# Seven block products for contraction steps 0 to 5 of the mix projection, a third weight sum on GpSimd

## The chip, the cores and the metric

One NeuronCore of a Trainium2 chip runs the whole program. The metric is the device time of one execution in microseconds (us). The kernel before was run three times; the profiled execution is a run of its own.

## The reference, cut to what matters

One decoder layer on 512 tokens and a model width of 1024, all in float32. The stage that changes is the last projection of the mixer, and the residual sum and norm behind it:

```python
merged = g[:, :, 0] * (o_a @ w_a) + g[:, :, 1] * (o_b @ w_b) + g[:, :, 2] * (o_c @ w_c)
return merged @ w_out
...
x = layer_norm(ALPHA * x + h, ln1_g[l], ln1_b[l])
h = memory_cross_attention(x, mem, w_xq[l], w_xkv[l], w_xo[l])
```

`merged` is 512 x 1024, `w_out` (`w_mix_out`) is 1024 x 1024. Every product is made in three matmuls: each float32 operand is split into a rounded part (`hi`) and the remainder (`lo`), and hi x hi, lo x hi and hi x lo are added up.

## The kernel before, in words

The layer is one program without a planner: each engine has its own written order, and semaphores tie the orders together. P = 128 rows are a tile; 512 tokens are four row blocks (t = 0 to 3), 1024 features are eight steps (k = 0 to 7).

Ahead of the mix run four gate iterations (`gate_iteration`, PE L2727, ACT L1279, DVE L1906). Each takes six gate pieces (q = 0 to 5) and two pieces of branch projections (q = 6, 7), every piece 24 matmuls of 512 columns. ScalarE rounds a weight piece of 1024 columns into `w_hi` (`gate_split`, L1305), VectorE makes the remainder into `w_lo` (`gate_rest`, L1901), TensorE multiplies, ScalarE takes the sigmoid into `sg`, and VectorE multiplies the three branches by their gates (L1922, L1923, L1929), adds them up (L1932, L1935) and splits the result into `m_hi` and `m_lo` (L1937, L1939), two steps k an iteration. A weight piece has a number p; `piece_done` counts the pieces that TensorE has used up, `lo_done` those whose remainder is made.

The mix product takes pieces PM to PM + 7, one for each step k. ScalarE rounds them (`split`, L1138), VectorE makes the remainders (`rest_of`, L1592), both on 1024 columns. TensorE (L2804 to L2827) begins with steps 0 and 1 over all row blocks, row blocks 2 and 3 first, since the last gated tiles are still being made, and then does steps 2 to 7 row block by row block (`rows_tail`, L2767). The product fills all eight PSUM banks, `2 * t + n` for row block t and column half n.

When a row block is complete, VectorE adds ALPHA times the residual input with a row sum (`norm_sums`, L1957), forms the mean (L1963), multiplies by gamma (`norm_gamma`, L1986), ScalarE sums the squares (L1321, L1324), GpSimd takes the root (L1112), and VectorE ends the norm (`norm_end`, L1995). TensorE then turns the normed block by eight small matmuls (`turn_tile`, L2437), ScalarE and VectorE split the turned tile into `xt_hi` and `xt_lo` (L1144, L1598). The turns of blocks 0 to 2 lie between the rows of later blocks, that of block 3 behind the memory keys (pieces PKX and PKX + 1, `tile_piece`, 24 matmuls of 256 columns each). Then come the cross attention's queries (`query`), which need the turned tiles.

SyncE issues all loads in one order (`load`, L886; the residual input L939; gamma and beta L941). Two raw buffers hold two pieces each. GpSimd has no work between the mixer's attention and the norms but the roots; in the first feed-forward product it makes one weight difference for each block (`weight_sums`, L1101).

The two feed-forward products are already made by seven block products. There `OUT_BANKS`, `out_slot` (half buffers of `w_hi` and `w_lo`), `LO` and `HI` (the lower and upper 256 tokens) and `OUT_PRODUCTS` are defined; the changed kernel uses them too. Some lines of the mix stage on TensorE:

```python
for k in range(2):
    pe.wait_ge(lo_done, PM + k + 1)
    for t in pair:
        for n in range(2):
            ins = rows_part(PM + k, k, t, n, m_hi, m_lo, k == 0, False)
...
rows_tail(PM, KT, N_TAIL, 0, m_hi, m_lo, lambda k: pe.wait_ge(merge_step, 6 * (k + 1)))
```

## Time and profile before

| what | value |
|---|---|
| three runs | 873.24, 873.60, 873.79 us; median 873.6 |
| profiled execution | 873.84 us, its span 872.1 us |
| TensorE (PE) matmul busy | 861.3 us, 99% of the span |
| VectorE (DVE) busy | 553.1 us, 63% |
| ScalarE (ACT) busy | 372.4 us, 43% |
| GpSimd (POOL) busy | 81.2 us, 9% |
| HBM traffic | 103 GB/s over the span |

The span runs from the first to the last instruction; 1.74 us of the device time lie around it. PE's matmuls overlap, so a matmul of 512 columns is shown with 389 ns, while the next one starts 227 ns after it: the pace is read from starts. In the timeline, `x2` marks two instructions merged into one row, and the bracket behind a row is the idle time before it with what ended it.

### The profile page before, as it was taken

The numbers are of one execution on the slowest core, as the hardware profiler recorded it, in microseconds if no ns is written. First come the engines' busy times: TensorE is split into PE (matmuls) and PEld (weight loads), VectorE is DVE, ScalarE is ACT, GpSimd is POOL, SyncE is SP. The second block draws the span as 40 slices with busy tenths as digits, with TensorE's granted clock in tenths as the row PEclk, the third lists the DMA queues.
The fourth block names the chain that finished last, engine by engine and source line by source line (L and its number), as shares of the span: only waits on it lengthen the run. The fifth ranks groups of instructions, "written<-read, shape, count | busy, mean of one in ns | idle before, by whom it ended". The sixth has DMA issues, their size and how long they took to land.

```text
span 872.1 us, 13309 instructions
## 1 busy us (share of the span) xinstructions
PE 861.3 (99%) x5143; PEld 747.3 (86%) x5143; DVE 553.1 (63%) x1016; ACT 372.4 (43%) x747; POOL 81.2 (9%) x103
## 2 busy tenths in 40 slices
PE   9999999999999999999999999999999999999996
PEld 8988888877678888888889979899999999888785
DVE  4344347769632626262767579679888888877934
ACT  4112157229642222222324554355656556434511
POOL 3100000081310000000000000011111111000000
PEclk9999999999999999999999999999999999999999
DMA  8534530430003333236531311313332333751101
GB/s 289 165 97 132 134 98 25 145 93 6 1 2 97 97 97 96 96 96 235 190 105 66 129 49 49 97 49 110 127 104 97 98 97 105 266 210 48 49 25 72
DMA packets 71832, 90.36 MB, mean 104 GB/s; under 512 B 3149, under 2 KB 62359, under 8 KB 71775
## 3 DMA queue, kind: packets, MB, share of 16 engines
q1 hardware_dynamic: 71391, 89.15, 31.3%
q8 instruction: 38, 0.62, 0.3%
q0 software_dynamic: 384, 0.43, 0.3%
q14 instruction: 19, 0.16, 0.1%
HBM read 87.05 MB, written 2.52 MB: 103 GB/s over the span
## 4 chain that ended last, share of the span: by engine, by line
PE 94%; DVE 3%; issue 1%; DMA 1%; ACT 1%; SPq 0%; DVEq 0%; POOLq 0%; POOL 0%; ACTq 0%
PE ps L2400 19%; PE ps L2402 19%; PE ps L2401 19%; PE ps L2970 7%; PE ps L2972 7%; PE ps L2971 7%; PE ps L2565 3%; PE ps L2642 3%; PE ps L2602 3%; PE ps L3028 1%; PE ps L3029 1%; PE ps L3030 1%; PE ps L2437 1%; DMA x_nat<-in_x 1%; PE ps L3073 1%
## 5 line engine op out<-in xcount | busy, mean ns | idle before, releaser
L2400 PE MATMUL ps<-xt_hi,w_hi 128*128 128x512 f32 (+1 forms) x400 | 155.6, 389 | 0.3 <-DVE w_lo L2110 0.3
L2402 PE MATMUL ps<-xt_lo,w_hi 128*128 128x512 f32 (+1 forms) x400 | 154.8, 387 | 0.0
L2401 PE MATMUL ps<-xt_hi,w_lo 128*128 128x512 f32 (+1 forms) x400 | 154.8, 387 | 0.0
L1138 ACT CAST w_hi<-raw 128x1024 fp32r<-128x1024 f32 (+1 forms) x49 | 50.5, 1035 | 133.3 <-PE ps L2402 121.6
L1901 DVE TENSOR_TENSOR w_lo<-raw,w_hi 128x1024 fp32r<-128x1024 f32 x30 | 36.7, 1224 | 90.1 <-ACT w_hi L1305 90.1
L2400 PEld LDWEIGHTS ps<-xt_hi,w_hi 128*128 128x128 f32 x400 | 75.1, 188 | 16.1 <-issue 1.1
L2402 PEld LDWEIGHTS ps<-xt_lo,w_hi 128*128 128x128 f32 x400 | 75.1, 188 | 15.4
L2401 PEld LDWEIGHTS ps<-xt_hi,w_lo 128*128 128x128 f32 x400 | 75.1, 188 | 15.1
L1592 DVE TENSOR_TENSOR w_lo<-raw,w_hi 128x1024 fp32r<-128x1024 f32 (+1 forms) x49 | 59.1, 1207 | 39.1 <-ACT w_hi L1138 38.9
L2971 PE MATMUL ps<-xt_hi,w_lo 128*128 128x256 f32 x288 | 81.5, 283 | 0.0
L2972 PE MATMUL ps<-xt_lo,w_hi 128*128 128x256 f32 x288 | 81.5, 283 | 0.0
L2970 PE MATMUL ps<-xt_hi,w_hi 128*128 128x256 f32 x288 | 81.5, 283 | 0.0
L2970 PE MATMUL ps<-s_hi,w_hi 128*128 128x256 f32 x216 | 61.3, 284 | 0.4 <-DVE w_lo L2144 0.3
L2971 PE MATMUL ps<-s_hi,w_lo 128*128 128x256 f32 x216 | 61.1, 283 | 0.0
L2972 PE MATMUL ps<-s_lo,w_hi 128*128 128x256 f32 x216 | 61.1, 283 | 0.0
L2144 DVE TENSOR_TENSOR w_lo<-raw,w_hi 128x512 fp32r<-128x512 f32 x72 | 49.9, 705 | 16.9 <-ACT w_hi L1416 16.6
L2971 PEld LDWEIGHTS ps<-xt_hi,w_lo 128*128 128x128 f32 x288 | 55.3, 192 | 0.1
L2970 PEld LDWEIGHTS ps<-xt_hi,w_hi 128*128 128x128 f32 x288 | 55.3, 192 | 0.1
L2972 PEld LDWEIGHTS ps<-xt_lo,w_hi 128*128 128x128 f32 x288 | 55.3, 192 | 0.0
L1291 ACT ACTIVATE sg<-ps,bias_t 128x512 f32<-128x512 f32 x24 | 16.6, 690 | 88.2 <-PE ps L2402 88.2
L1416 ACT CAST w_hi<-raw 128x512 fp32r<-128x512 f32 x72 | 44.3, 622 | 7.8 <-PE ps L2972 4.5
L1101 POOL TENSOR_TENSOR w_t<-raw 128x512 f32<-128x512 f32 x18 | 28.7, 1594 | 176.2 <-DMA raw<-in_w_ffn_in 151.9
(391 smaller groups left out, 1979.1 us busy)
## 6 DMA issues: line engine op xcount, KB each, us to landing
raw<-in_w_in SPq DMA_DIRECT2D x24, 1024.0 KB, 5.0
raw<-in_w_ffn_in SPq DMA_DIRECT2D x36, 512.0 KB, 4.4
raw<-in_w_ffn_out SPq DMA_DIRECT2D x7, 1024.0 KB, 4.8
raw<-in_w_mix_out SPq DMA_DIRECT2D x4, 1024.0 KB, 4.9
raw<-in_w_ffn_in SPq DMA_DIRECT2D x4, 1024.0 KB, 5.3
out_w<-in_w_ffn_out SPq DMA_DIRECT2D x4, 1024.0 KB, 8.8
raw<-in_w_branch_b SPq DMA_DIRECT2D x4, 512.0 KB, 3.9
resid<-in_x SPq DMA_DIRECT2D x1, 2048.0 KB, 9.5
```

Of the source, the lines that this page charges most:

```text
L1101: pool.tensor_tensor(w_t1[:, :, :], w_quarter(n, 0, 1), w_quarter(n, 0, 0), ALU.subtract).then_inc(t1_done, 1)
L1138: act.copy(hi, src).then_inc(hi_done, 1)
L1416: act.copy(op_slot(m, 0), right_operand(kind, n)).then_inc(op_hi, 1)
L1592: dve.tensor_tensor(lo, src, f32(hi), ALU.subtract).then_inc(lo_done, 1)
L1901: dve.tensor_tensor(w_lo[s][:, :].rearrange("p (k c) -> p k c", k=KT), v, f32(w_hi[s][:, :]).rearrange("p (k c) -> p k c", k=KT), ALU.subt ...
L2144: dve.tensor_tensor(op_slot(m, 1), right_operand(kind, n), f32(op_slot(m, 0)), ALU.subtract).then_inc(op_lo, 1)
L2400: pe.matmul(dst, a_hi, b_hi, start=start, stop=False, skip_group_check=reopened)
L2401: pe.matmul(dst, a_lo, b_hi, start=False, stop=False, skip_group_check=reopened)
L2402: return pe.matmul(dst, a_hi, b_lo, start=False, stop=stop, skip_group_check=reopened)
L2970: pe.matmul(dst, w_h[:, k, :], x_h[:, k, :], start=clear and k == 0, stop=False, skip_group_check=True)
L2971: pe.matmul(dst, w_l[:, k, :], x_h[:, k, :], start=False, stop=False, skip_group_check=True)
L2972: ins = pe.matmul(dst, w_h[:, k, :], x_l[:, k, :], start=False, stop=k == 3, skip_group_check=True)
```

## The change

Steps 0 to 5 of the contraction are no longer eight block products of (256 tokens x 3 steps) by (3 steps x 512 columns), but seven. Even steps (0, 2, 4) are the first block row of the weight, odd steps the second. Sums of the left blocks (S1 to S4, rounded into `n1`, `n3`, `n2` and in place of the block of P3) are made on VectorE and ScalarE in the last gate iteration, when steps 0 to 5 of `m` are complete. Four quarters of the weight rows 0 to 767 come by loads of their own into `mix_b` and `mix_w`. VectorE makes the weight sums T1, T2 and the fourth (into T2's place), 1536 columns each; GpSimd makes the third, T3, in three parts of 512 columns, once P5's remainders are made. Each right part of 512 columns is rounded by ScalarE (`mix_round`) and gets its remainder from VectorE (`mix_rest`), 21 of each in place of six pieces of 1024 columns. Between products ScalarE copies two banks into two others twice (`mix_seeds`, `mix_second_seeds`); VectorE adds the banks of P5 and P6/P7 to ALPHA times the residual (`keep_scaled`), so the last column half's norm sum takes the residual unscaled. Steps 6 and 7 stay plain (`rows_tail` over two steps) and P4 comes between the row blocks 1 and 2. On VectorE the last gate iteration is written out: its gate products go into `sg`, and its adds and splits stand between the remainders. On SyncE the residual load waits for P1's remainders and the third weight sum, gamma and beta for P7. The turn of block 2 moves behind the first memory-key piece, and `rest_of(PKX)`, `rest_of(PKX + 1)` and `rest_of(PXQ)` move into the norms. Piece numbers and waits behind the mix are renumbered.

```diff
+        MIX_T1 = raw[0][:, 0:N_MIX * 512].rearrange("p (k c) -> p k c", k=N_MIX)
+        MIX_B11, MIX_B12 = mix_b[:, 0, :, :], mix_b[:, 1, :, :]
+        MIX_B22, MIX_B21, MIX_T2, MIX_T3 = (mix_w[:, i, :, :] for i in range(4))
+        MIX_RIGHT = {"P1": MIX_B11, "P2": MIX_B21, "P3": MIX_B22, "P5": MIX_T1, "P6": MIX_T2, "P7": MIX_T3, "P4": MIX_T2}
...
+            sp.wait_ge(m_sum_lo, 4)
+            mix_quarter(MIX_B12, 0, 1).then_inc(mix_in, 16)
+            mix_quarter(MIX_B11, 0, 0).then_inc(mix_in, 16)
+            sp.wait_ge(piece_done, (N_PAIR - 1) * 8 + PG + 6)
+            mix_quarter(MIX_B22, 1, 1).then_inc(mix_in2, 16)
+            mix_quarter(MIX_B21, 1, 0).then_inc(mix_in2, 16)
             for c in range(CM, CF):
+                if c == CM + 1:
+                    sp.wait_ge(mix_lo, mix_op("P1", N_MIX))
+                    sp.wait_ge(mix_t3, N_MIX)
+                    sp.dma_start(resid[:, :, :], A["x"][0].rearrange("(t p) n -> p t n", p=P)).then_inc(resid_in, 16)
+                    sp.wait_ge(mix_lo, mix_op("P5", N_MIX))
                 load(c)
-                if c == CM:
-
-                    sp.wait_ge(o_ab_lo, N_OUT_AB)
-                    sp.wait_ge(o_lo_done, KT - N_OUT_AB)
-                    sp.dma_start(resid[:, :, :], A["x"][0].rearrange("(t p) n -> p t n", p=P)).then_inc(resid_in, 16)
+                if c == CM + 1:
+                    sp.wait_ge(mix_prod, mix_op("P7", N_MIX))
...
+            pool.wait_ge(mix_lo, mix_op("P5", N_MIX))
+            for k in range(N_MIX):
+                pool.tensor_tensor(MIX_T3[:, k, :], MIX_B22[:, k, :], MIX_B12[:, k, :], ALU.subtract).then_inc(mix_t3, 1)
...
+                if m < 4:
+                    act.wait_ge(piece_done, PM - 1 + m // 2)
+                else:
+                    act.wait_ge(mix_prod, m - 3)
+                act.copy(out_slot(m, 0), MIX_RIGHT[kind][:, k, :]).then_inc(mix_hi, 1)
...
+            for kind in OUT_PRODUCTS:
+                for k in range(N_MIX):
+                    if (kind, k) != ("P1", 0):
+                        mix_round(kind, k)
+                    if kind == "P7" and k in (0, 2):
+                        split(PM + k // 2)
+                if kind == "P5":
+                    mix_seeds()
+                if kind == "P2":
+                    mix_second_seeds()
...
+            m_add(M_D, "P4")
+            m_add(M_C, "P3")
+            dve.wait_ge(m_whole, 2)
+            dve.tensor_tensor(M_D, M_C, M_D, ALU.add).then_inc(m_sum, 1)
+            m_add(M_A, "P1")
+            gate_rest(LAST_I, 3, 0)
+            dve.wait_ge(m_whole, 3)
+            dve.tensor_tensor(M_C, M_A, M_C, ALU.subtract).then_inc(m_sum, 1)
+            dve.wait_ge(m_sum, 2)
+            dve.tensor_tensor(M_A, M_D, M_A, ALU.subtract).then_inc(m_sum, 1)
+            m_add(M_B, "P2")
+            dve.wait_ge(m_whole, 4)
+            dve.wait_ge(m_sum, 3)
+            dve.tensor_tensor(M_B, M_B, M_A, ALU.subtract).then_inc(m_sum, 1)
+            gate_rest(LAST_I, 4, 0)
+            for kind in ("P5", "P7", "P6", "P3"):
+                m_rest(kind)
+            gate_rest(LAST_I, 5, 0)
...
+            dve.wait_ge(mix_in, 32)
+            dve.wait_ge(lo_done, 8 * LAST_I + PG + 6)
+            dve.tensor_tensor(MIX_T1, MIX_B12, MIX_B11, ALU.subtract).then_inc(mix_t, 1)
+            gate_rest(LAST_I, 7, 0)
+            dve.wait_ge(piece_done, PM - 1)
+            dve.wait_ge(sig_done, N_PAIR * 6)
+            gate_product(6, 0).then_inc(merge_step, 1)
+            gate_product(7, 2).then_inc(merge_step, 1)
+            gate_product(0, 4).then_inc(merged_even, 1)
+            mix_rest("P1", 0)
+            mix_rest("P1", 1)
+            dve.wait_ge(mix_in2, 32)
+            dve.wait_ge(mix_t, 1)
+            dve.tensor_tensor(MIX_T2, MIX_B22, MIX_T1, ALU.subtract).then_inc(mix_t, 1)
+            dve.wait_ge(piece_done, PM)
+            gate_product(2, 3).then_inc(merge_step, 1)
+            mix_rest("P1", 2)
+            gate_product(1, 1).then_inc(merge_step, 1)
+            gate_product(3, 5).then_inc(merged_odd, 1)
+            for k in range(N_MIX):
+                mix_rest("P5", k)
+            for k in range(N_MIX):
+                mix_rest("P6", k)
+            dve.wait_ge(merge_step, merged_so_far + 4)
+            dve.wait_ge(merged_even, N_PAIR)
+            add_gated(0, True)
+            dve.wait_ge(merge_step, merged_so_far + 5)
+            add_gated(0, False)
+            mix_rest("P2", 0)
+            split_gated(0)
+            mix_rest("P2", 1)
+            dve.wait_ge(merged_odd, N_PAIR)
+            add_gated(1, True)
+            mix_rest("P2", 2)
+            dve.wait_ge(merge_step, merged_so_far + 9)
+            add_gated(1, False)
+            dve.wait_ge(mix_lo, mix_op("P6", N_MIX))
+            dve.tensor_tensor(MIX_T2, MIX_B21, MIX_T2, ALU.subtract).then_inc(mix_t, 1)
+            mix_rest("P7", 0)
+            rest_of(PM)
+            mix_rest("P7", 1)
+            split_gated(1)
+            mix_rest("P7", 2)
+            dve.wait_ge(resid_in, 16)
+            dve.wait_ge(mix_prod, mix_op("P5", N_MIX))
+
+            def keep_scaled(t, bank):
+
+                v = resid[:, t, 512:1024]
+                dve.scalar_tensor_tensor(out=v, in0=v, scalar=ALPHA, in1=ps[:, bank, :], op0=ALU.mult,
+                                         op1=ALU.add).then_inc(mix_kept, 1)
+
+            for r in range(2):
+                keep_scaled(r, 5 + 2 * r)
+            mix_rest("P3", 0)
+            rest_of(PM + 1)
+            mix_rest("P3", 1)
+            mix_rest("P3", 2)
+            dve.wait_ge(mix_prod, mix_op("P7", N_MIX))
+            for r in range(2):
+                keep_scaled(2 + r, 4 + 2 * r)
+            for k in range(N_MIX):
+                mix_rest("P4", k)
...
             norm_sums(0)
-            norm_out(0)
+            norm_gamma(0)
+            rest_of(PKX)
+            norm_end(0)
             norm_sums(1)
-            norm_out(1)
+            norm_gamma(1)
+            rest_of(PKX + 1)
+            norm_end(1)
             turn_tile(1, 0)
             norm_sums(2)
             norm_out(2)
             turn_tile(1, 1)
-            norm_sums(3, (0,))
+            norm_sums(3)
+            norm_gamma(3)
+            rest_of(PXQ)
+            norm_end(3)
             turn_tile(1, 2)
-            norm_sums(3, (1,))
-            norm_out(3)
-            rest_of(PXQ)
             rest_of(PXQ + 1)
...
+                def part(k, r):
+
+                    m = mix_op(kind, k)
+                    pe.wait_ge(mix_lo, m + 1)
+                    w_h, w_l = out_slot(m, 0), out_slot(m, 1)
+                    rows = slice(P * r, P * r + P)
+                    dst = ps[:, OUT_BANKS[kind][r], :]
+                    clear = kind in ("P1", "P5") and k == 0
+                    pe.matmul(dst, x_h[:, k, rows], w_h, start=clear, stop=False, skip_group_check=True)
+                    pe.matmul(dst, x_l[:, k, rows], w_h, start=False, stop=False, skip_group_check=True)
+                    return pe.matmul(dst, x_h[:, k, rows], w_l, start=False, stop=k == N_MIX - 1, skip_group_check=True)
+
+                if kind == "P1":
+                    for k in range(N_MIX):
+                        part(k, 0)
+                    pe.wait_ge(merge_step, 2 * N_PAIR * 6 - 9)
+                    for k in range(N_MIX):
+                        part(k, 1).then_inc(mix_prod, 1)
                 else:
-                    pe.wait_ge(merged_odd, N_PAIR)
-                for k in range(2):
-                    pe.wait_ge(lo_done, PM + k + 1)
-                    for t in pair:
-                        for n in range(2):
-                            ins = rows_part(PM + k, k, t, n, m_hi, m_lo, k == 0, False)
-                    if pair[0] == 0:
-                        ins.then_inc(piece_done, 1)
-            rows_tail(PM, KT, N_TAIL, 0, m_hi, m_lo, lambda k: pe.wait_ge(merge_step, 6 * (k + 1)))
-            rows_tail(PM, KT, N_TAIL, 1, m_hi, m_lo)
+                    for k in range(N_MIX):
+                        part(k, 0)
+                        part(k, 1).then_inc(mix_prod, 1)
+
+            for kind in OUT_PRODUCTS[:-1]:
+                mix_product(kind)
+            mixed = PM - 2 * N_MIX
+            rows_tail(mixed, KT, KT - 2 * N_MIX, 0, m_hi, m_lo,
+                      lambda k: pe.wait_ge(merge_step, 2 * N_PAIR * 6 - 4 * (KT - 1 - k)))
+            rows_tail(mixed, KT, KT - 2 * N_MIX, 1, m_hi, m_lo)
+            mix_product(OUT_PRODUCTS[-1])
             turn_tile(1, 0)
-            rows_tail(PM, KT, N_TAIL, 2, m_hi, m_lo)
+            rows_tail(mixed, KT, KT - 2 * N_MIX, 2, m_hi, m_lo)
             turn_tile(1, 1)
-            rows_tail(PM, KT, N_TAIL, 3, m_hi, m_lo, halves=(0,))
-            rows_tail(PM, KT, N_TAIL, 3, m_hi, m_lo, halves=(1,), part=slice(0, 2))
-            turn_tile(1, 2)
-            rows_tail(PM, KT, N_TAIL, 3, m_hi, m_lo, halves=(1,), part=slice(2, None))
+            rows_tail(mixed, KT, KT - 2 * N_MIX, 3, m_hi, m_lo)
 
             pe.wait_ge(mem_lo, 4)
             pe.wait_ge(turn_lo, 2 * TT + 2)
             for n in range(2):
                 pe.wait_ge(lo_done, PKX + n + 1)
                 tile_piece(PKX + n, n, memt_hi, memt_lo, slice(0, MEM))
+                if n == 0:
+                    turn_tile(1, 2)
             turn_tile(1, 3)
```

## Rows read from the trace of the kernel before

**Rows 1.** The page: granted clock by slice, and the chain that ended last.
```profile
PEclk9999999999999999999999999999999999999999
...
PE 94%; DVE 3%; issue 1%; DMA 1%; ACT 1%; SPq 0%; DVEq 0%; POOLq 0%; POOL 0%; ACTq 0%
```
**Rows 2.** PE's groups by form, 420.96 to 474.1: count | busy us, mean ns | idle.
```profile
L2400 PE MATMUL ps<-x_hi,m_hi 128*128 128x512 f32 x32 | 12.7, 398 | 0.0
```
**Rows 3.** PE in order of time, mix to queries: start, duration in us, line.
```profile
420.97 0.39 PE L2400 MATMUL ps<-w_hi,m_hi 128*128 128x512 f32 x1
421.19 0.39 PE L2401 MATMUL ps<-w_hi,m_lo 128*128 128x512 f32 x1
...
423.46 0.39 PE L2402 MATMUL ps<-w_lo,m_hi 128*128 128x512 f32 x1
423.87 0.50 PE L2400 MATMUL ps<-w_hi,m_hi 128*128 128x512 f32 x1
...
467.56 0.28 PE L2400 MATMUL ps<-memt_hi,k_hi 128*128 128x256 f32 x1
...
474.11 0.36 PE L2400 MATMUL ps<-xt_hi,c_hi 128*128 128x256 f32 x1
```
**Rows 4.** DVE in order of time, the last two merges.
```profile
416.93 1.22 DVE L1592 TENSOR_TENSOR w_lo<-raw,w_hi 128x1024 fp32r<-128x1024 f32 x1
418.07 0.68 DVE L1929 TENSOR_TENSOR mt<-ps,sg 128x512 f32<-128x512 f32 x1
418.67 0.68 DVE L1932 TENSOR_TENSOR mt<-mt 128x512 f32<-128x512 f32 x1
419.38 0.69 DVE L1935 TENSOR_TENSOR mt<-mt 128x512 f32<-128x512 f32 x1
420.11 0.43 DVE L1937 CAST m_hi<-mt 128x512 fp32r<-128x512 f32 x1
420.57 0.69 DVE L1939 TENSOR_TENSOR m_lo<-mt,m_hi 128x512 fp32r<-128x512 f32 x1
...
422.60 1.22 DVE L1592 TENSOR_TENSOR w_lo<-raw,w_hi 128x1024 fp32r<-128x1024 f32 x1
```
**Rows 5.** DMA issues, KB, us to landing; first three issued at 402.3 to 404, last 475.5.
```profile
raw<-in_w_mix_out SPq DMA_DIRECT2D x1, 1024.0 KB, 4.9
...
resid<-in_x SPq DMA_DIRECT2D x1, 2048.0 KB, 9.5
...
gb<-in_ln_b SPq DMA_DIRECT2D x1, 512.0 KB, 11.6
...
gb<-in_ln_b SPq DMA_DIRECT2D x1, 512.0 KB, 7.7
```
**Rows 6.** POOL in order of time, first feed-forward product.
```profile
591.53 1.30 POOL L1101 TENSOR_TENSOR w_t<-raw 128x512 f32<-128x512 f32 x1 [6.82 <-DMA raw<-in_w_ffn_in]
601.78 1.71 POOL L1101 TENSOR_TENSOR w_t<-raw 128x512 f32<-128x512 f32 x1 [8.95 <-DVE w_lo L2144]
```
**Rows 7.** DVE in order of time at the same places.
```profile
591.57 1.81 DVE L2158 TENSOR_TENSOR w_t<-raw,w_t 128x512 f32<-128x512 f32 x1
...
601.65 0.68 DVE L2194 TENSOR_TENSOR h_lo<-ht,h_hi 128x512 fp32r<-128x512 f32 x1
602.25 1.78 DVE L2158 TENSOR_TENSOR w_t<-raw,w_t 128x512 f32<-128x512 f32 x1
```
**Rows 8.** DVE in order of time: the norms of row blocks 2 and 3.
```profile
457.79 0.69 DVE L1957 SCALAR_TENSOR_TENSOR resid<-resid,ps 128x512 f32<-128x512 f32 x1 [2.74 <-PE ps L2402]
...
458.77 1.28 DVE L1986 SCALAR_TENSOR_TENSOR norm_part<-resid,neg_mean,gb 128x1024 f32<-128x1024 f32 x1
461.02 1.28 DVE L1995 SCALAR_TENSOR_TENSOR resid<-norm_part,rstd,gb 128x1024 f32<-128x1024 f32 x1 [0.96 <-POOL rstd L1112]
462.22 1.28 DVE L1598 TENSOR_TENSOR xt_lo<-ps,xt_hi 128x512 fp32r<-128x512 f32 x2
...
471.01 1.28 DVE L1995 SCALAR_TENSOR_TENSOR resid<-norm_part,rstd,gb 128x1024 f32<-128x1024 f32 x1 [0.99 <-POOL rstd L1112]
```

More of the change, by code:

```diff
@@ L1284, in gate_iteration @@
                     if last and q == 7:
-                        split(PM)
+                        mix_round("P1", 0)
                     elif not (first and q == 0):
                         gate_split(i, np_ - PG, wrap)
+                    if last and q == 3:
+                        for kind in ("P5", "P7", "P6", "P3"):
+                            m_round(kind)
                     if q < 6:
@@ L1310, in _ @@
             gate_iteration(N_PAIR - 1, True)
-            for p in range(PM + 1, PM + 8):
-                split(p)
+            for kind in OUT_PRODUCTS:
[6 more added lines that the diff above has]
+                    mix_seeds()
+                if kind == "P2":
+                    mix_second_seeds()
             act.wait_ge(merge_step, 2 * N_PAIR * 6)
@@ L1939, in gate_iteration, with m_add @@
                         dve.tensor_tensor(ml, mt[:, 0, :], f32(mh), ALU.subtract).then_inc(merge_step, 1)
-            gate_iteration(0, False)
+            gate_iteration(0)
             with dve.Fori(1, N_PAIR - 1) as i:
-                gate_iteration(i, False)
-            gate_iteration(N_PAIR - 1, True)
+                gate_iteration(i)
+            M_A, M_B, M_C, M_D = (m_sums[:, i, :, :] for i in range(4))
+            LAST_I = N_PAIR - 1
+            def m_add(dst, kind):
+                dve.tensor_tensor(dst, f32(m_left(kind, 0)), f32(m_left(kind, 1)), ALU.add).then_inc(m_whole, 1)
@@ L1956, in norm_sums @@
                     v = resid[:, t, c * 512:(c + 1) * 512]
-                    dve.scalar_tensor_tensor(out=v, in0=v, scalar=1.0 if n >= 2 * TT else ALPHA, in1=ps[:, 2 * t + c, :],
+                    scaled = n >= 2 * TT or n < TT and c == 1
+                    dve.scalar_tensor_tensor(out=v, in0=v, scalar=1.0 if scaled else ALPHA, in1=ps[:, 2 * t + c, :],
                                              op0=ALU.mult, op1=ALU.add,
@@ L2011, in turn_tile @@
                     turn_drain(2 * t + hf, 2 * TT * k + 2 * t + hf)
-            for p in range(PM + 2, PKX + 2):
-                rest_of(p)
             def memory_key_out(n):
```

156 lines of the change are left out of this document (125 added, 31 removed).

## The prediction

> **What bounds the kernel now.** I read the page first: TensorE holds 94% of the chain that ended last, at a granted clock of 9 tenths or more in every slice [rows 1]; the table above has it busy 99% of the span. So one question decides: how long TensorE takes from its first mix matmul to the first query matmul. What follows is untouched and moves with it. The groups of TensorE's lines in that stretch show six groups of mix matmuls like the one here, 6 x 32 = 192 [rows 2]. TensorE's order of time gives the ends: the mix begins at 420.97, the memory keys at 467.56, the queries at 474.11, 53.1 us in all [rows 3]. Matmuls with 512 columns start 0.227 us apart (420.97, 421.19). There is one stall: from 423.46 to 423.87, where 0.227 is due, behind the VectorE subtraction that ended at 422.60 + 1.22 = 423.82 [rows 3, 4]. It and the slow starts after it cost 0.3; about 0.12 of that is the restart itself, my price for each further one.
>
> **What goes.** The plain product has 192 matmuls. The changed one has 7 products x 3 steps x 2 row halves x 3 = 126, and keeps 2 x 4 x 2 x 3 = 48 for steps 6 and 7, together 174. 18 x 0.227 = 4.1 us go, and the old stall of 0.3: with nothing in its way TensorE would need 53.1 - 4.4 = 48.7 us.
>
> **What comes, walked engine by engine.** VectorE's durations, start to start: an operation on 512 columns 0.60 (418.07 to 418.67), on 1024 columns 1.14 (416.93 to 418.07), so 0.87 for 768 and 1.67 for 1536; one that needs the result before it 0.71 (418.67 to 419.38); a copy of 512 columns 0.46 (420.11 to 420.57) [rows 4].
>
> *Last gate iteration, 384 to 421.* Eight sums of 768 columns and four remainders come onto VectorE, 12 x 0.87 = 10.4 us, and four roundings onto ScalarE. VectorE has one rest of 1.14 in each 5.44 us of TensorE there (24 matmuls), so they fit between. The two pairs of weight quarters are 1.5 MB each; 1 MB landed after 4.9 us, 2 MB behind another 1 MB after 9.5 [rows 5]. Asked for at about 400.4 and 410.3 and priced between, at 7.2, they are in at 407.6 and 417.5; wanted at 407.7 and 418.7; at 9.5 only the second is late, and by 0.3 past the pause that follows. Taken at nothing.
>
> *Start of the mix.* P1's third right part can be rounded only when the last gate piece leaves its slot, 421.15, and VectorE first has a gate product (to 421.8). The part is there at 422.5, wanted at 422.3. Cost 0.2.
>
> *GpSimd's sums.* P5's last remainder ends at 426.2 and releases three GpSimd subtractions of 512 columns. Alone one takes 1.30 (591.53) [rows 6]. What it does beside VectorE stands in the trace: VectorE's subtraction of two SBUF tensors at 591.57 takes 1.81 where 0.69 is usual, the one at 602.25 takes 1.78, and GpSimd's of 601.78 (1.71) had itself stood behind VectorE's of 601.65 [rows 6, 7]. So a subtraction with two SBUF inputs loses 1.12 us when a GpSimd one has just begun, and the engines take turns. VectorE has only such work then: remainders for P6, adds, remainders for P2. The first GpSimd sum (426.3 to 427.5) falls into a pause of VectorE; the second and third (begun about 428.0 and 429.7) each hold up a remainder. Cost on VectorE 2 x 1.12 = 2.2.
>
> The Trainium skill (SBUF — State Buffer, section "SBUF: two separate sides") calls the port pair of VectorE and GpSimd an exclusive lock, held for a whole instruction, against VectorE operations with two SBUF inputs too. By that rule the sums cost the same 2.2, and the trace agrees (1.81 against 0.69); if the engines did not block each other it would be nothing, the first rival.
>
> *To P7.* From 427.4 VectorE has no pause: P6's remainders 1.8, two adds 1.3, P2's remainders 1.8, the even gate's split 1.1, two adds 1.2, the fourth sum 1.7, P7's first remainder 0.7, together 9.6. It ends at 427.4 + 2.2 + 9.6 = 439.2. One part of P2 is 0.2 late on the way. TensorE wants P7's at 420.97 + 4 x 4.08 + 0.2 + 0.2 + two restarts = 438.0. Cost 0.2 + 1.2.
>
> *P7 and P3.* Between six remainders VectorE has two rests of 1.14, a split of 1.1 and two scaled keeps of 0.6. By these durations four parts come 0.25, 0.2, 0.3 and 0.25 late. Cost 1.0. The restarts so far, seven at 0.12, are 0.8. The first keep also waits for the residual input, whose load now stands behind the third GpSimd sum: asked for at 431.0, it takes 4.9 to 9.5 [rows 5], so it is in by 440.5, wanted at 442.5. Covered by 2 us. The first cross-attention load queues behind it on SyncE's queue (431.5, wanted at 448.5), the second behind gamma and beta (445.5, wanted at 466.8); behind GpSimd's sums stands only the first norm's root (454). All covered.
>
> *The norms.* TensorE ends the first block of plain rows at 420.97 + 6 x 4.08 + 9 x 0.227 + the stalls 2.6 + restarts 0.8, and 0.2 for the last matmul to run out = 451.1. From there VectorE has for each row block: two sums and a mean 1.6 (0.61, then 457.79 to 458.77), gamma 1.3 (458.77 takes 1.28), the end 1.2 (461.02 to 462.22) [rows 8], 4.1 in all, four times 16.5; three weight rests that the change puts in between, 3.4; two turned tiles of two halves, 2.4; one wait for the root, 0.96 (461.02) [rows 8]. That is 23.3 us without a pause: the last block is normed at 474.4. TensorE's own way from the same matmul: 0.7 for the other half of block 0, 2.7 for block 1, P4 4.1, 5.4 for blocks 2 and 3, and for memory keys and turns what they took before: 6.55 from 467.56 to 474.11 with one turn of 0.8 [rows 3], so 5.75 and three turns 2.4, together 21.1, and 0.1 for slow starts, from 450.9 to 472.1. Before, VectorE ended its last norm at 471.01 + 1.28 = 472.3, a turn (0.8) and a full 1.0 ahead of the query at 474.11 [rows 3, 8]. Now it is the later one. Cost 2.2. The first query also needs the low part of the third tile, which VectorE makes only after that norm: 0.2, and a restart 0.1.
>
> Gamma and beta are asked for when P7 ends, the second at 444.8. It landed 7.7 us after its issue with 1 MB ahead, 11.6 with 3 MB ahead [rows 5]; nothing is queued ahead of it now, so I take at most 7.7: in by 452.5, wanted at 452.9. Counted at nothing; each microsecond over is paid in full.
>
> **Sum.** 48.7 + 0.2 + 0.2 + 1.2 + 1.0 + 0.8 + 2.2 + 0.2 + 0.1 = 54.6. Some ten hand-overs between engines are in the walk at 0.03; the one of 423.82 to 423.87 is 0.05, so 0.2 more: 54.8. Against 53.1 that is +1.7. The profiled execution took 873.84 us (span 872.1 and 1.74 around it), 0.24 above the median of the three runs, 873.6. 873.84 + 1.7 = 875.5; against the median it would be 875.3.
>
> **Rivals.** *GpSimd costs nothing.* Its sums fall into pauses or do not block: P7 begins on time and all that follows is 1.9 us earlier, 873.6, no change. Against it the rows of 1.8 us; for it, that no row has three GpSimd operations in a row.
> *VectorE keeps up.* If its lane through the norms is 2 us shorter than counted and P7 and P3 get their parts in time, 0.2 to 1.5 us of stalls are left: 873.84 - 4.4 + 1.5 = 871. For it: TensorE's chain share of 94% shows helpers hidden nearly everywhere, and the lane is long, so small errors add up. Against it: the lane is counted from rows, and it has no pause to lose.
> *A late load* (slower by a mechanism of its own). VectorE waits in order for the residual and for gamma and beta, with every remainder and norm queued behind. It decides if the residual takes over 11.5 us, or gamma and beta over 8.1 from the second issue, 0.4 above the row. At the 11.6 once seen it is 3.5 late: 879; at half of that 877.5.
> *Steps 0 to 5 stay eight products.* The code's loops say otherwise; under 1 in 100.
>
> **How the numbers follow.** Forecast 875.5: 0.50, its own range 874.4 to 876.9. GpSimd free, 873.6: 0.20. VectorE keeps up, 871: 0.15. Late load, 877.5 to 879: 0.15. Leaving out about a tenth at either end: 872.2 to 878.3. This kernel can be told from no change by about 0.2%, 1.75 us: faster is below 871.85, slower above 875.35. Of the forecast's 0.50 some 0.32 lies above 875.35; with the late load slower is 0.47. Faster is 0.14 of the 0.15. No difference is the rest, 0.39.
>
> **What would show it.** In the changed profile: VectorE subtractions of about 1.8 us near 428 to 431 beside GpSimd's; TensorE idle some 1.2 us before P7's first part, behind VectorE; tenths before P7's and P3's later parts; about 2.2 us before the last turn, behind the last norm's end; the queries at about 475.8. If no subtraction there exceeds 0.7, GpSimd is free. If gamma's row is late with a DMA as releaser, it is the late load. If TensorE idles under 2 us in all between 421 and 475, I counted VectorE too long and the forecast is wrong.

## The result, and the profile after

The changed kernel takes 879.53 us (median of four runs, 878.64 to 880.22) against 873.69 of the kernel before on the same chip: a ratio of 1.0062, 95% interval [1.0046, 1.0078]. It is slower by 5.8 us. The forecast was 875.5, with a range up to 878.3. The profiled execution took 878.64 us, its span is 876.9.

The page of the changed kernel, its chain that ended last by engine (before: [rows 1]):

```profile
PE 87%; DVE 7%; issue 2%; ACT 2%; DMA 1%; POOL 1%; SPq 0%; DVEq 0%; POOLq 0%; ACTq 0%
```

TensorE held 94% of the chain and now holds 87%; VectorE went from 3% to 7%. The kernel lost time not in matmuls but in waits for VectorE. TensorE in order of time, changed kernel: start, duration in us, line, and in brackets the idle time and its releaser (before: [rows 3]):

```profile
421.06 0.39 PE L3064 MATMUL ps<-w_hi,m_hi 128*128 128x512 f32 x1
...
438.19 0.39 PE L3066 MATMUL ps<-w_lo,m_hi 128*128 128x512 f32 x1
439.74 0.47 PE L3064 MATMUL ps<-w_hi,n_hi 128*128 128x512 f32 x1 [1.16 <-DVE w_lo L2073]
...
463.72 1.09 PE L2672 MATMUL ps<-ident,resid 128*128 128x128 f32 x8 [0.98 <-DVE resid L2228]
...
476.99 1.09 PE L2672 MATMUL ps<-ident,resid 128*128 128x128 f32 x8 [2.79 <-DVE resid L2228]
478.19 0.39 PE L2635 MATMUL ps<-xt_hi,c_hi 128*128 128x256 f32 x1
```

From the first mix matmul to the first query TensorE took 420.97 to 474.11, 53.1 us. Now it is 421.06 to 478.19, 57.1 us: 4.0 more, where 1.7 were forecast. The three bracketed waits hold 4.9. The last two have the end of a norm (L2228) as releaser. VectorE of the changed kernel (before: [rows 4, 8]):

```profile
427.40 4.51 DVE L2073 TENSOR_TENSOR w_lo<-mix_w,w_hi 128x512 fp32r<-128x512 f32 x3 [0.90 <-ACT w_hi L1397]
...
437.24 1.75 DVE L2151 TENSOR_TENSOR mix_w<-mix_w 128x1536 f32<-128x1536 f32 x1
438.91 0.68 DVE L2073 TENSOR_TENSOR w_lo<-mix_w,w_hi 128x512 fp32r<-128x512 f32 x1
...
454.75 1.23 DVE L1706 TENSOR_TENSOR k_lo<-raw,k_hi 128x1024 fp32r<-128x1024 f32 x1
456.53 1.28 DVE L2228 SCALAR_TENSOR_TENSOR resid<-norm_part,rstd,gb 128x1024 f32<-128x1024 f32 x1 [0.55 <-POOL rstd L1176]
```

And all that GpSimd does there: the third weight sum and four roots (its work of the same kind before: [rows 6]):

```profile
426.67 4.70 POOL L1166 TENSOR_TENSOR mix_w<-mix_w,mix_b 128x512 f32<-128x512 f32 x3 [182.12 <-DVE w_lo L2073]
454.90 1.52 POOL L1176 TENSOR_TENSOR rstd<-var,half 128x1 f32<-128x1 f32 x1 [23.53 <-ACT var L1438]
460.87 1.40 POOL L1176 TENSOR_TENSOR rstd<-var,half 128x1 f32<-128x1 f32 x1 [4.45 <-ACT var L1438]
467.91 0.55 POOL L1176 TENSOR_TENSOR rstd<-var,half 128x1 f32<-128x1 f32 x1 [5.65 <-ACT var L1438]
474.14 1.40 POOL L1176 TENSOR_TENSOR rstd<-var,half 128x1 f32<-128x1 f32 x1 [5.68 <-ACT var L1438]
```

The reader is to see one column. A root works on one element per partition. In norm 2 it takes 0.55; in norms 0, 1 and 3, where a remainder of 1024 columns (L1706) runs on VectorE, it takes 1.40 to 1.52, and VectorE then waits for it, 0.55 at 456.53. The loads that the prediction feared came in time (KB, us to landing; before: [rows 5]):

```profile
resid<-in_x SPq DMA_DIRECT2D x1, 2048.0 KB, 8.9
...
gb<-in_ln_g SPq DMA_DIRECT2D x1, 512.0 KB, 3.9
gb<-in_ln_b SPq DMA_DIRECT2D x1, 512.0 KB, 5.2
```

### The profile page after: what moved, and what is told of

Its sections match the earlier page's. It is cut to its first block, busy times and chain, and to the rows that moved or that the text cites. A ratio compares the mean times of both kernels' runs of the same rounds, so it can differ in the third digit from the quotient of the medians.

```text
span 876.9 us, 13358 instructions
## 1 busy us (share of the span) xinstructions
PE 859.7 (98%) x5125; PEld 743.0 (85%) x5125; DVE 581.7 (66%) x1050; ACT 383.3 (44%) x770; POOL 91.3 (10%) x106
## 4 chain that ended last, share of the span: by engine, by line
PE 87%; DVE 7%; issue 2%; ACT 2%; DMA 1%; POOL 1%; SPq 0%; DVEq 0%; POOLq 0%; ACTq 0%
PE ps L2635 18%; PE ps L2637 17%; PE ps L2636 17%; PE ps L3234 6%; PE ps L3236 6%; PE ps L3235 6%; PE ps L2800 3%; PE ps L2877 3%; PE ps L2837 2%; PE ps L3292 1%; PE ps L3294 1%; PE ps L3293 1%; DVE w_lo L2073 1%; DMA x_nat<-in_x 1%; ACT squares L1435 1%
## 5 line engine op out<-in xcount | busy, mean ns | idle before, releaser
L1204 ACT CAST w_hi<-raw 128x1024 fp32r<-128x1024 f32 (+1 forms) x45 | 46.4, 1034 | 121.5 <-PE ps L2637 113.4
L1706 DVE TENSOR_TENSOR w_lo<-raw,w_hi 128x1024 fp32r<-128x1024 f32 (+1 forms) x45 | 54.0, 1200 | 35.9 <-ACT w_hi L1204 35.6
L1160 POOL TENSOR_TENSOR w_t<-raw 128x512 f32<-128x512 f32 x18 | 30.8, 1714 | 174.1 <-DMA raw<-in_w_ffn_in 131.4
```

Of the source, the lines that this page charges most:

```text
L1160: pool.tensor_tensor(w_t1[:, :, :], w_quarter(n, 0, 1), w_quarter(n, 0, 0), ALU.subtract).then_inc(t1_done, 1)
L1204: act.copy(hi, src).then_inc(hi_done, 1)
L1706: dve.tensor_tensor(lo, src, f32(hi), ALU.subtract).then_inc(lo_done, 1)
```

## The experiments

Two lengths are read from each trace, because they are free of what happens earlier and later: from the first mix matmul to the first query, and on to the first matmul of the cross-attention scores (`kx,qx`). The times are medians; each ratio is taken against the kernel before on the same chip (medians there 873.64 to 873.91).

| kernel | mix to query | mix to scores | median us | ratio to before, 95% |
|---|---|---|---|---|
| before | 53.14 | 63.37 | 873.69 | 1 |
| changed | 57.13 | 67.40 | 879.53 | 1.0062 [1.0046, 1.0078] |
| the same, twice more | 57.15, 57.14 | 68.90, 68.90 | 879.59, 879.85 | 1.0064 [1.0050, 1.0078], 1.0071 [1.0057, 1.0084] |
| e1 no third sum | 55.10 | 66.57 | 877.77 | 1.0044 [1.0030, 1.0058] |
| e2 third sum on VectorE | 55.15 | 65.41 | 876.82 | 1.0040 [1.0026, 1.0053] |
| e3 rests out of the norms | 56.56 | 66.80 | 879.31 | 1.0067 [1.0053, 1.0081] |
| e4 rests ahead of gamma | 56.38 | 66.64 | 878.76 | 1.0058 [1.0043, 1.0074] |
| e5 query ahead of last turn | 53.98 | 66.16 | 876.92 | 1.0038 [1.0024, 1.0052] |
| e6 = e2 and fourth sum late | 54.30 | 64.56 | 876.56 | 1.0031 [1.0018, 1.0045] |
| e7 = e4 (norms 0, 1), e5 and e6 | 50.62 | 62.80 | 873.68 | 0.9999 [0.9990, 1.0008] |
| e8 = e7, new order of the norms | 48.94 | 60.07 | 871.56 | 0.9974 [0.9965, 0.9983] |
| e9 changed, with that order | 51.93 | 63.05 | 874.28 | 1.0007 [0.9998, 1.0016] |
| e10 changed, idle time filled | 57.13 | 67.39 | 878.04 | 1.0047 [1.0033, 1.0061] |

In e5, e7, e8 and e9 the last turn (0.8 us) stands behind the first query piece, so for them the second column is the one to compare.

**The changed kernel again**, beside e1 to e3 and, as a control, beside e10.

> The changed kernel as it is, once more, as the yardstick for the runs beside it. 878.6 to 880.3 us, 5 to 6.5 us above the kernel before. From its first trace the queries begin 4.1 us later than before (478.19 against 474.11), and 0.55 us more came from one late weight load near 749 us; if that load was chance, its median should be nearer to 878 than to 880.

> The changed kernel as it stands, once more, on the chip of e10_filled, as its control: about half of its executions at 878.6 to 879.1 and half at 880.0 to 880.5, the upper ones with a stretch at 0.5 clock behind the last turn; median 879.5.

Medians 879.59 and 879.85: the result repeats. The control missed its expectation of two groups: its five executions lie between 879.33 and 880.60 and none near 878.7. What both traces have that the first did not is told under e10.

**e1: the third sum is left out.** The seventh product then multiplies by the plain quarter, which is not the reference's product, and the residual load waits for P6's remainders instead.

```diff
-            for k in range(N_MIX):
-                pool.tensor_tensor(MIX_T3[:, k, :], MIX_B22[:, k, :], MIX_B12[:, k, :], ALU.subtract).then_inc(mix_t3, 1)
...
-        MIX_RIGHT = {..., "P7": MIX_T3, ...}
+        MIX_RIGHT = {..., "P7": MIX_B22, ...}
```

> Leaves out the third weight sum: P7 takes the plain quarter in its place, GpSimd does nothing there, and the residual load waits for P6's remainders instead. Theory that GpSimd holds VectorE up: the three P6 remainders, 4.51 us in the changed kernel, take 1.9; TensorE's wait of 1.3 us before P7's first part goes, and of the tenths before P7's and P3's later parts nothing changes; the queries begin 1.6 to 2.1 us earlier, 477.5 to 478 us in all. Rival, VectorE's amount of work alone makes it late and GpSimd costs under 0.5: within 0.5 us of the changed kernel.

**e2: the third sum on VectorE**, one part behind P5's first remainder, two behind its last, ahead of P6's. Same arithmetic, 1.9 us more work on the busier engine.

```diff
+            mix_rest("P5", 0)
+            third_sum(0)
+            mix_rest("P5", 1)
+            mix_rest("P5", 2)
+            third_sum(1)
+            third_sum(2)
```

> The third weight sum on VectorE in place of GpSimd, three parts of 512 columns, the first behind P5's first remainder, the others behind its third, where VectorE paused for 0.66 and 0.90 us. Theory of the hold-up: VectorE has 1.8 us more of work and loses no 2.6 to GpSimd, of the 1.8 about 1.3 falls into the pauses; faster than the changed kernel by 1.5 to 2.2 us. Rival, amount of work: slower than it by 0.3 to 1.8.

Both shorten mix to query by 2.0 us. The medians fall by 1.8 and 2.8 against the repeat; the second is more than the 1.5 to 2.2 forecast. In e2 TensorE's wait before P7 is gone: 0.40 from start to start where 1.55 stood, and 0.23 is due:

```profile
438.39 0.39 PE L3069 MATMUL ps<-w_lo,n_hi 128*128 128x512 f32 x1
438.79 0.50 PE L3067 MATMUL ps<-w_hi,n_hi 128*128 128x512 f32 x1
```

So GpSimd's sum does not cost by the work in it but by what it holds up. VectorE reaches the adds behind P6's remainders 8.75 us after the first mix matmul in e1, 8.78 in e2 and 10.78 in the changed kernel (431.84). The sum costs VectorE 2.0 us on GpSimd and nothing in its own pauses. (In e1 the three remainders still take 2.4 and not the 1.9 forecast, since 0.51 of a wait for ScalarE's rounding shows up between them.) That is not the whole loss: e2 still has the 2.78 us wait before the last turn, and three of its four roots take 1.40 to 1.52.

**e3: the weight rests out of the norms**: the two of the memory keys ahead of the first norm's sums, the query's behind the last norm.

```diff
+            rest_of(PKX)
+            rest_of(PKX + 1)
             norm_sums(0)
-            norm_gamma(0)
-            rest_of(PKX)
-            norm_end(0)
+            norm_out(0)
```

> The three weight rests that the change put between gamma and the end of norms 0, 1 and 3 are taken out: two before the first norm's sums, that of the query weights behind norm 3. Theory that a rest beside GpSimd's root holds the root up (1.40 to 1.52 us in the changed kernel where it is 0.55): the roots take 0.55 again, a norm from gamma to end 2.25 in place of 3.1, three times 0.85 shorter; the second rest before the sums costs about 1.0, the query weights' rest behind the last norm 1.1 before the queries. The last turn comes 1.2 to 1.6 us earlier, the queries 0 to 0.6 us earlier. Rival, the roots are long for another reason (one row block's variance late): roots stay at 1.4 and the last turn does not come earlier.

GpSimd in e3, first and last root, and TensorE's last turn:

```profile
455.04 0.58 POOL L1176 TENSOR_TENSOR rstd<-var,half 128x1 f32<-128x1 f32 x1 [24.29 <-ACT var L1438]
...
472.56 0.55 POOL L1176 TENSOR_TENSOR rstd<-var,half 128x1 f32<-128x1 f32 x1 [5.67 <-ACT var L1438]
```

```profile
474.59 1.09 PE L2669 MATMUL ps<-ident,resid 128*128 128x128 f32 x8 [1.98 <-DVE resid L2228]
```

All four roots are back at 0.55 to 0.58, so it was the remainders that held them. But the median does not move (879.31). The trace says one half of why: with the query's rest behind the last norm, VectorE makes it while TensorE waits for the query, so of 1.8 us won at the last turn (474.59 is 54.1 behind the first mix matmul, 476.99 is 55.9) only 0.6 is left at the query. The other half is in the executions that no trace shows: the profiled one took 877.18 us at a mean granted clock of 0.997, the other four 879.08 to 880.09 at 0.994 and 0.995. What that clock stands for is told under e10.

**e4: the same rests, ahead of the gamma product** in norms 0, 1 and 3.

```diff
             norm_sums(0)
-            norm_gamma(0)
             rest_of(PKX)
+            norm_gamma(0)
             norm_end(0)
```

> The changed kernel, with each remainder that stands between a norm's gamma product and its end moved ahead of the gamma product (norms 0, 1 and 3). VectorE then subtracts while ScalarE squares, and the root of GpSimd falls on the gamma product (scalar_tensor_tensor) in place of the remainder (tensor_tensor). Theory A: only the tensor_tensor remainder holds GpSimd's 128x1 operation. Then the three roots take 0.55 us in place of 1.40 to 1.52, the norm ends come without a wait, three times 0.5 earlier, the last turn is issued some 1.6 us earlier than 476.99, and the time falls to 877.5 to 878.3. Theory B: any VectorE instruction over 1024 columns holds it, scalar_tensor_tensor too. Then the roots stay at 1.4 or come up to 1.28 later still, the last norm ends where it did or later, and the time is 879.0 to 880.5.

The root does not go back to 0.55. VectorE and GpSimd of e4, norm 0:

```profile
453.30 1.21 DVE L1706 TENSOR_TENSOR k_lo<-raw,k_hi 128x1024 fp32r<-128x1024 f32 x1
454.44 1.28 DVE L2219 SCALAR_TENSOR_TENSOR norm_part<-resid,neg_mean,gb 128x1024 f32<-128x1024 f32 x1
```

```profile
454.98 1.17 POOL L1176 TENSOR_TENSOR rstd<-var,half 128x1 f32<-128x1 f32 x1 [23.53 <-ACT var L1438]
```

The remainder was over at 454.44. What the root began beside, and outlasted by 0.4, is the gamma product. Theory B is right about the mechanism: the gamma product holds it too, a scalar_tensor_tensor with two inputs in SBUF. That any VectorE instruction would, one with a single SBUF input too, no run here shows. It is wrong about the price: the last norm's end begins 23.1 us behind the start of the first sums, 0.8 earlier than in the changed kernel (23.9), and the median (878.76) lies between the two forecasts. The Trainium skill (SBUF — State Buffer, section "Who interferes with whom") says that a VectorE instruction with two SBUF inputs contends with a GpSimd instruction that reads SBUF, whoever comes second being blocked entirely. The traces agree for both forms, and show that it holds for a GpSimd instruction of a single column: 1.14 to 1.52 against 0.55.

**e5: the first query piece ahead of the last turn.** It needs tokens 0 to 255 only, whose turns are done long before; ScalarE and VectorE split the third turned tile, and VectorE makes the query's rest, ahead of the last norm's gamma product.

```diff
             query(0, 0)
+            turn_tile(1, 3)
             query(0, 1)
```

> The changed kernel, with the first query piece of tokens 0 to 255 ahead of the last turn of tokens on TensorE, which needs only the turns before it; VectorE drains the third turn and makes the first query remainder ahead of the last norm's gamma product. The weight sum on GpSimd and the three stages ahead of norm 3 are as in the changed kernel. Theory (the norm lane is what TensorE waits for in the end, and the low clock follows from that idle time): the first query starts at about 475.1 in place of 478.2, the idle time of 2.8 us ahead of the last turn falls to 1 us or less, the scores start near 486.2 in place of 488.46, no execution has a stretch of 0.5 clock there, and the time is 876.3 to 877.2, with a spread under 1 us between executions. Rival (the offset of 4.1 us is set in the product itself and by what feeds it, and the queries are held by something else, such as VectorE's own queue): the time stays at 878.7 to 880.3.

TensorE in e5:

```profile
474.54 0.36 PE L2635 MATMUL ps<-xt_hi,c_hi 128*128 128x256 f32 x1 [0.84 <-DVE c_lo L1706]
477.48 1.03 PE L2672 MATMUL ps<-ident,resid 128*128 128x128 f32 x8
482.25 0.36 PE L2635 MATMUL ps<-xt_hi,c_hi 128*128 128x256 f32 x1 [0.87 <-issue]
```

The wait for the last norm is gone: the turn at 477.48 has no bracket. The scores come 1.2 earlier (67.40 to 66.16), not the 2.3 expected, because of a new wait of 0.87 at 482.25. Its line names no releaser. VectorE's order does: the drain of the first query (L2258) starts at 481.73, behind a rest and the memory keys' drain, and the query at 482.25 overwrites that bank. In e8 that drain is moved up, and the wait is gone. The median, 876.92, is in the forecast range; the spread of 2.0 us between executions is not the "under 1" forecast, though all five have a mean granted clock of 0.997 to 0.999, so something else than the clock scatters too.

**e6: third sum on VectorE, and the fourth sum late**, behind P3's remainders, as only P4 needs it.

```diff
-            dve.tensor_tensor(MIX_T2, MIX_B21, MIX_T2, ALU.subtract).then_inc(mix_t, 1)
             mix_rest("P7", 0)
...
             mix_rest("P3", 2)
+            dve.tensor_tensor(MIX_T2, MIX_B21, MIX_T2, ALU.subtract).then_inc(mix_t, 1)
```

> The run before with the third sum on VectorE, and beside that the fourth sum (1.75 us, VectorE) moved from ahead of the seventh product's remainders to behind the third block product's. Theory: what is left of TensorE's hold-ups between 438 and 446 (about ten starts 0.1 to 0.3 late, together 1.2 us) comes from VectorE being late by the length of that sum; they go, and sum 0 of the norms comes at 447.9 to 448.3 in place of 449.18. The time is 875.3 to 876.2. Rival: the hold-ups come from the four split slots alone (ScalarE's copy waits for TensorE to be done with a slot); they stay, and the time stays at 876.6 to 877.5. Second rival: the last product's remainders come too late behind the moved sum, with a wait of TensorE ahead of the last product's first part (about 452).

PE's groups by form between 437 and 447, P7's first matmul of each part: e2, then e6.

```profile
L3067 PE MATMUL ps<-w_hi,n_hi 128*128 128x512 f32 x6 | 2.6, 427 | 0.0
```

```profile
L3067 PE MATMUL ps<-w_hi,n_hi 128*128 128x512 f32 x6 | 2.3, 389 | 0.0
```

A matmul that restarts shows as a longer one (427 ns on average); with the fourth sum out of the way all six take the usual 389. Mix to scores falls by 0.85. VectorE now reaches the first norm's sums at 448.36 with no pause before them; that, not TensorE's rows, is where the gain stops. The profiled execution (875.49) is in the theory's range; the median, 876.56, is 0.4 above it.

**e7: all of this together.**

> All together: third sum on VectorE, fourth sum late, the remainders ahead of the gamma product in norms 0 and 1, and the first query piece ahead of the last turn. Theory: the parts add up, 2.8 (third sum) + 1 (fourth sum) + 2.3 (query first) and, if the remainders hold GpSimd's root and the gamma product does not, up to 1 more: 872.0 to 874.5, so the change would be level with the kernel before or a little faster. Rival: the norm lane of VectorE takes back what the product gains, and the time stays above 875.

873.68: level with the kernel before, its scores 0.6 earlier. The parts add up at the scores, 4.6 earlier than in the changed kernel: 2.0 and 0.85 from the two sums, 1.2 from the first query (e5) and 0.5 from norms 0 and 1 (e4). The forecast had larger terms, 2.8, 1 and 2.3; the median falls by 5.85, more than the scores, since the low clock told under e10 is gone too. The drain of the first query still costs 0.87.

**e8: the norms in an order in which VectorE seldom waits for a root**, and the drain of the first query ahead of the last turn's remainder. The lines are against e7.

```diff
             norm_gamma(0)
+            norm_sums(1)
             norm_end(0)
-            norm_sums(1)
             rest_of(PKX + 1)
             norm_gamma(1)
             norm_end(1)
-            turn_tile(1, 0)
             norm_sums(2)
+            turn_tile(1, 0)
             norm_gamma(2)
...
+            query_out(0, 0)
             turn_tile(1, 3)
```

> The run e7_all with VectorE's order between the norms written anew, so that none of its instructions waits for a root: the sums of norm 1 between norm 0's gamma product and its end, the first turn's remainder between the sums and the gamma product of norm 2, the first query's remainders between those of norm 3, and the drain of the first query ahead of the last turn's remainder. Same instructions, another order. Theory (VectorE's lane of norms is the bound from 449 on, 2.1 us of it is waits for roots, and 0.9 us of TensorE's wait at the query of tokens 256 to 511 is the late drain): turn 1 comes without a wait, the first query at about 469.5 in place of 471.34, the scores at 480.5 to 481.5 in place of 483.52, and the time is 870.5 to 871.8, under both kernels. Rival (the seven products give nothing that later stages keep, because a load or the exponentials of the cross-attention set their pace): the scores come earlier but the time stays at 873 to 874.

TensorE in e8, at the first turn, the second, the last and before it the first query:

```profile
455.44 1.03 PE L2676 MATMUL ps<-ident,resid 128*128 128x128 f32 x8
...
459.05 1.04 PE L2676 MATMUL ps<-ident,resid 128*128 128x128 f32 x8
...
469.46 0.38 PE L2639 MATMUL ps<-xt_hi,c_hi 128*128 128x256 f32 x1
...
472.44 1.04 PE L2676 MATMUL ps<-ident,resid 128*128 128x128 f32 x8
```

No bracket is left from 449 to the scores. The roots still take 1.15 to 1.20 there; VectorE does other work meanwhile (one wait of 0.55, in norm 2, is left). 871.56 us, 0.9974 [0.9965, 0.9983] of the kernel before: the seven products are worth 2.1 us once VectorE feeds them. Its scores come 3.3 earlier than before, and its profiled execution is 3.0 shorter (870.84 against 873.84); 0.4 of the 3.3 is lost in the second feed-forward product (see the next part). Why the medians keep only 2.1 no trace shows.

**e9: that order alone, on the changed kernel.** GpSimd keeps the third sum.

> The changed kernel with that order of VectorE's norms and of TensorE's queries alone: the third sum stays on GpSimd and the fourth sum stays ahead of the seventh product's remainders. Theory: what the product loses by these two (sum 0 at 451.3 in place of 448.65) passes through the norms in full once no wait for a root hides it, so the scores come 2.6 later than in e8_lane_all and the time is 873.0 to 874.5, level with the kernel before. Then the order of the norms is worth 5 to 6 us to the changed kernel, more than the two sums (2.6). Rival (the slack of the norms takes the 2.6 up): under 872.5.

874.28, in the theory's range; the rival under 872.5 is out. Its scores come 0.3 earlier than before's and its median is 0.6 above, which this measurement cannot tell from none (the interval holds 1). Against e8 the scores come 3.0 later: what the product stage loses is passed on in full. It was so in the old order too: from the changed kernel to e6 the same two sums move the scores by 2.84 (67.40 to 64.56). VectorE's lane through the norms had no slack to take them up in either order. The order of the norms is worth 4.35 us to the changed kernel (67.40 to 63.05), the place of the two sums 3.0.

**e10: TensorE's idle time filled.** The control's trace has something that no row of the first has. PE's windows in the control: window, PE busy and matmuls, granted clock, DMA share and GB/s.

```profile
476.00:477.00 1.00, 0.29 (x3) 1.00 0.00 0
477.00:478.00 1.00, 0.90 (x9) 1.00 0.00 0
478.00:479.00 1.00, 1.00 (x7) 0.76 0.00 0
479.00:480.00 1.00, 1.00 (x7) 0.50 0.00 0
480.00:481.00 1.00, 1.00 (x6) 0.50 0.95 131
481.00:482.00 1.00, 1.00 (x6) 0.53 0.99 401
482.00:483.00 1.00, 1.00 (x11) 1.00 1.03 426
```

Behind the 2.8 us without a matmul the granted clock is 0.50 for some 3 us: 1.2 GHz in place of 2.4. TensorE is busy all the time, but with 6 or 7 matmuls in a microsecond, not 11. Two starts at the full clock, two at half:

```profile
478.25 0.28 PE L2637 MATMUL ps<-xt_lo,c_hi 128*128 128x256 f32 x1
478.37 0.28 PE L2635 MATMUL ps<-xt_hi,c_hi 128*128 128x256 f32 x1
...
479.30 0.41 PE L2637 MATMUL ps<-xt_lo,c_hi 128*128 128x256 f32 x1
479.52 0.41 PE L2635 MATMUL ps<-xt_hi,c_hi 128*128 128x256 f32 x1
```

That is 0.12 against 0.22, and from query to scores 11.76 us against 10.27, 1.5 lost. The edit puts matmuls with a product that nobody reads into the wait:

```diff
+            for i in range(20):
+                pe.matmul(ps[:, 2, 0:MEM], k_hi[:, 1, 0:P], memt_hi[:, i % KT, 0:MEM], start=True, stop=True)
             turn_tile(1, 3)
```

> The changed kernel, with 20 matmuls of 256 columns, whose product nobody reads, into a free bank while TensorE waits for the last turn (2.4 us of 2.8). Nothing else is changed and no wait is shortened. Theory (the stretch at 0.5 clock behind the last turn follows from that idle time): no stretch at 0.5 is left, the executions lie together, 878.5 to 879.4, and none at 880 or over. Rival (the low clock comes by chance, or from the load of the stretch ahead of it, whatever TensorE does there): about half of the executions still lie at 880.0 to 880.5, 1.4 above the others.

Windows of e10 at the same place:

```profile
477.00:478.00 1.00, 0.60 (x5) 1.00 0.00 0
478.00:479.00 1.00, 0.89 (x9) 1.00 0.00 0
479.00:480.00 1.00, 1.00 (x8) 1.00 0.00 0
480.00:481.00 1.00, 1.00 (x11) 1.00 0.00 0
```

The mix to query is the changed kernel's to 0.01, the clock stays, and the five executions lie at 877.05 to 878.89 against 879.33 to 880.60 of the control beside it. The median and two more of the five lie below the 878.5 to 879.4 forecast; none is at 880, so the rival is out. Adding useless work to a stretch where TensorE waited made the kernel 1.8 us faster at the median, of which at most the 1.5 above can be the clock. The two profiled executions differ by only 0.5 (878.89 and 879.38), since in e10's the mix began 1.05 us later (421.82 against 420.77), upstream of the edit.

The mean granted clock of each execution says roughly how often this happens. In every trace the clock is 0.50 for the last 1 to 5 us, behind the last matmul; with that alone the mean is 0.997 to 0.999 (eleven traces), and with a stretch at 0.50 in mid-kernel too it is 0.995 or 0.996 (three traces). By that mark, at least 28 of the 38 executions of the kernels with 2.0 to 2.8 us of idle time before the last turn (the changed one, its two repeats, e1 to e4 and e6) had such a stretch, 11 of 14 of the changed kernel itself, and none of the 43 of e5 and e7 to e10, nor any of the kernel before beside them (55). The profiled execution of the changed kernel (0.997) is one of the few without it; e3, with 1.98 us of idle time, has it in four of five.

## Why the prediction was wrong

The direction was right, and so was most of the walk; the size was not.

- *What goes.* Right. 126 mix matmuls and 48 of plain rows, as counted. With VectorE in time the saving is there: at the scores e8 gains 3.3 of the 4.4 us.
- *Start of the mix, 0.2.* Right: 0.29 (422.20 to 422.72, where 0.23 is due).
- *GpSimd's sums, 2.2 on VectorE.* Right: 2.0 by e1 and e2. The three remainders took 4.51.
- *P7's first part, 1.2.* Right: 438.19 to 439.74 is 1.3 over the usual start. VectorE's remainder was forecast ready at 439.2 and was at 439.5.
- *P7's and P3's parts, 1.0 and restarts.* Right: starts of 0.40 to 0.52 where 0.23 is due, four times, 0.9 together. The first norm's sums began 30.7 us behind the first mix matmul, forecast were 30.1.
- *The norms, 23.3 us on VectorE.* This is the step that failed. From 451.75 to the last norm's end at 475.65 + 1.28 = 476.93 it was 25.2: 1.9 more. The prediction gave each of the three weight rests its 1.14 us, took the waits for the roots in norms 0, 1 and 3 as gone behind them, and kept one wait for a root, 0.96. It had itself found that a subtraction with two SBUF inputs and a GpSimd instruction exclude each other [rows 6, 7], and used this for the sums of 512 columns, but did not apply it to the roots, which are GpSimd work on SBUF too; of them it wrote only that the first stands behind the sums in GpSimd's queue. The change had moved the rests to just where the roots fall. Each of the three roots took 0.85 to 0.97 longer and VectorE waited 0.55, 0.53 and 0.52 for it: 1.6 of the 1.9 missing. e3 shows the cause, e4 that moving them a place does not cure it. The rest, 0.3, has no row of its own.
- *From the last norm to the query, 1.4.* Right: 1.3.
- *"What follows is untouched and moves with it."* False; this is the second step that failed, a term put at nothing. The wait before the last turn, which the prediction had forecast as 2.2 and which was 2.8, was followed by the low clock in three of seven traces that have 2.6 to 2.8 us of idle time there (the control, the repeat and e1; not the first, e2, e4 and e6) and, by the mean clocks under e10, in 11 of the changed kernel's 14 executions. It cost 1.2 to 1.5 from query to scores. No trace without such a wait shows it, and e10 takes it away. The four times do not sort by it alone: 878.64 has a mean clock of 0.997, and 878.96, 880.09 and 880.22 have 0.995 or 0.996. The other part is weight loads of the second feed-forward product. In the profiled execution ScalarE waited 0.53 for one at 749.43, and between 700 and 765 the offset to before grew from 4.2 to 4.8. In the repeat it grew by 1.0 there, in the control by 0.1, in the other traces by -0.1 to 1.3. This looks like scatter of the loads, but there is only one trace of the kernel before, so that the change has no part in it is not shown.
- *The rivals.* (Half of the late load's 3.5 us on 875.5 is 877.3, not the 877.5 given; nothing hangs on it.) GpSimd free: false, e2. VectorE keeps up: false for this kernel, true for e8. Late load: false, the residual in 8.9 us and beta in 5.2, where 11.5 and 8.1 would have been needed. Slower came, but not by the mechanism that the rival on that side had.

The sum, then: 4.0 from mix to query in place of 1.7 (0.56 in the product stage, 1.9 in the norms, -0.1 behind them), 1.2 to 1.5 from the clock in most executions, and 0.1 to 1.0 in the second feed-forward product, together about the 5.8 of the median. The last two are read from traces of single executions; how the median divides between them is an estimate.

What stays open: when idle time of this length brings the clock down and when not, and what makes the loads of the second feed-forward product late. It was not tried whether the kernel before gains by the order of e8; between 421 and 474 its TensorE has but the one stall of [rows 3], so no wait of that stretch is there to be won.

## What to carry to other kernels

Before an engine gets new work, list every instruction that the neighbour it can exclude (here GpSimd for VectorE) has in that stretch, the one-element ones too: it is not their length that counts but who waits for them. A rest put "into the pause" of a wait can lengthen the wait. When a change takes work from the bounding engine and gives it to its feeder, walk the feeder's order to the next stage, and reorder there first: here the same seven products are 5.8 us slower or 2.1 us faster by the order of VectorE's instructions, the place of TensorE's first query and one sum's engine.

## What the hardware showed that was not expected

- A GpSimd instruction on 128 x 1 elements takes 0.55 us alone and 1.14 to 1.52 when a VectorE instruction of 1024 columns with two SBUF inputs, tensor_tensor or scalar_tensor_tensor, has begun before it; it ends about 0.4 behind VectorE's.
- Three remainders of 512 columns beside three GpSimd subtractions took 4.51 us; alone three take 1.89:

```profile
446.28 1.89 DVE L2068 TENSOR_TENSOR w_lo<-mix_w,w_hi 128x512 fp32r<-128x512 f32 x3
```

- After 2.8 us without a matmul in the middle of a kernel TensorE's granted clock fell to 0.50 in three traces, 0.5 to 1.8 us after the matmuls had begun again, for some 3 us; in four traces with 2.6 to 2.8 us it did not. The Trainium skill (TensorE: Matmul & The Clock Gate, "Part 1: The HAM clock gate") says that the low clock is the resting state and activity lifts it. The traces agree in so far as filling the wait with matmuls kept the clock up (e10). They add that the same kernel meets the low clock in some executions and not in others.
